# Second down projection in four groups of seven block products, with the weight sums made in HBM by GpSimd's transfers

## The reference

```python
x = x + jnp.concatenate([a, p], axis=-1) @ w_out[l]
h2 = rms_norm(x, norm2_g[l])
x = x + (jax.nn.silu(h2 @ w_gate[l]) * (h2 @ w_up[l])) @ w_down[l]
```

## Time and profile before

| what | us |
|---|---|
| median of three runs | 802.08 (802.04 to 802.59) |
| the profiled execution | 801.26 |
| its span | 799.8 |
| PE busy in the span | 793.5 |
| DVE, ACT, POOL busy | 625.5, 456.3, 88.8 |
| second down projection, from its first to its last matmuls | 57.3 |

### The profile page before, as it was taken

How to read it: one execution, slowest core, us unless ns; L and a number is a source line. 1 busy time by engine, 2 the same in 40 slices (tenths; PEclk the granted TensorE clock), 3 DMA queues, 4 the chain that set the end, 5 groups by cost and what they waited for, 6 DMA issues and landing times.

```text
span 799.8 us, 13164 instructions
## 1 busy us (share of the span) xinstructions
PE 793.5 (99%) x5158; PEld 696.3 (87%) x5158; DVE 625.5 (78%) x1037; ACT 456.3 (57%) x738; POOL 88.8 (11%) x77
## 2 busy tenths in 40 slices
PE   8999999999999999999999999999999999999998
PEld 6888888999888888899999998887778888888886
DVE  6889998785555766679999997486866898787977
ACT  6676677454535544456656563456665566555552
POOL 0001000010011202101101110011100333011100
PEclk9999999999999999999999999999999999999999
DMA  9655564557433556475687655464425666884321
GB/s 316 189 166 169 178 228 146 143 146 226 126 116 96 173 168 202 163 240 179 192 253 242 224 187 209 162 206 161 156 79 148 198 207 213 291 285 159 108 101 55
DMA packets 118126, 144.09 MB, mean 180 GB/s; under 512 B 11553, under 2 KB 86705, under 8 KB 117809
## 3 DMA queue, kind: packets, MB, share of 16 engines
q1 hardware_dynamic: 115616, 141.22, 54.9%
q10 hardware_dynamic: 2448, 2.03, 1.1%
HBM read 141.78 MB, written 1.46 MB: 179 GB/s over the span
## 4 chain that ended last, share of the span: by engine, by line
PE 97%; DVE 1%; DMA 1%; issue 0%; ACT 0%; SPq 0%; DVEq 0%; ACTq 0%
PE bank L654 94%; PE bank L770 1%; DMA panel_raw<-in_w_in 1%; DVE conv_acc L1788 1%; PE bank L1090 0%; PE bank L814 0%; PE bank L1039 0%; DVE panel_lo L1752 0%; PE bank L1063 0%; PE bank L867 0%; PE bank L792 0%; PE bank L969 0%; SPq L2607 0%; ACT panel_hi L1236 0%; DVE h L2213 0%
## 5 line engine op out<-in xcount | busy, mean ns | idle before, releaser
L1752 DVE TENSOR_TENSOR panel_lo<-panel_raw,panel_hi 128x1024 fp32r<-128x1024 f32 x237 | 299.9, 1268 | 109.2 <-ACT panel_hi L1236 107.2
L654 PE MATMUL bank<-x_halves,panel_hi 128*128 128x256 f32 (+1 forms) x1536 | 366.9, 321 | 0.7 <-DVE x_halves L2220 0.7
L1236 ACT ACTIVATE panel_hi<-panel_raw 128x1024 fp32r<-128x1024 f32 (+1 forms) x239 | 251.9, 1055 | 154.2 <-PE bank L654 152.1
L654 PE MATMUL bank<-x_halves,panel_lo 128*128 128x256 f32 x1024 | 288.3, 282 | 0.0
L654 PEld LDWEIGHTS bank<-x_halves,panel_hi 128*128 128x128 f32 x1536 | 255.8, 190 | 23.3 <-issue 0.9
L654 PEld LDWEIGHTS bank<-x_halves,panel_lo 128*128 128x128 f32 x1024 | 194.9, 190 | 0.2
L654 PE MATMUL bank<-panel_hi,x_halves 128*128 128x512 f32 x384 | 122.1, 399 | 0.0
L654 PEld LDWEIGHTS bank<-panel_hi,x_halves 128*128 128x128 f32 x384 | 70.0, 188 | 14.1 <-issue 0.3
L654 PE MATMUL bank<-panel_lo,x_halves 128*128 128x512 f32 x192 | 75.1, 391 | 0.0
L654 PE MATMUL bank<-panel_hi,act_hi 128*128 128x512 f32 x156 | 60.9, 390 | 0.0
L654 PE MATMUL bank<-panel_hi,act_lo 128*128 128x512 f32 x156 | 60.7, 389 | 0.0
(11 more groups left out here) (312 smaller groups left out, 1011.2 us busy)
## 6 DMA issues: line engine op xcount, KB each, us to landing
panel_raw<-in_w_in SPq DMA_DIRECT2D x35, 1024.0 KB, 5.3
panel_raw<-in_w_up SPq DMA_DIRECT2D x30, 1024.0 KB, 5.4
panel_raw<-in_w_down SPq DMA_DIRECT2D x16, 1024.0 KB, 5.0
panel_raw<-in_w_gate SPq DMA_DIRECT2D x10, 1024.0 KB, 5.5
panel_raw<-in_w_out SPq DMA_DIRECT2D x8, 1024.0 KB, 5.0
panel_raw<-in_w_in SPq DMA_DIRECT2D x11, 512.0 KB, 4.8
panel_raw<-in_w_branch_fox SPq DMA_DIRECT2D x4, 1024.0 KB, 5.0
panel_raw<-in_w_branch_gdn SPq DMA_DIRECT2D x4, 1024.0 KB, 5.0
```

What stands on the lines that cost most here:

```text
L654: return e.matmul(o, l, r, start=start, stop=stop, skip_group_check=True)
L1236: return e.activation(o, i_, ACT.Copy, scale=scale)
L1752: e.tensor_tensor(lo, raw_view(i, k0, kt), hi.bitcast(F32), ALU.subtract).then_inc(s_lo, 1)
```

## The change

There are four groups in place of two, so 16 of the 22 k-tiles are done by block products and 6 by plain halves. `HALVES` grows from 258 to 264, the list of panels shrinks from 130 to 126. `GROUP_ORDER` sets the seven products of a group without plain halves between them; a plain half stands ahead of each of the first two groups and four stand at the end.

DVE's adds of weight blocks are gone. The sums are made in HBM, in a scratch array `weight_sums`, by transfers that POOL issues: `copied` writes a block there, `added` accumulates another onto it. Each group has four stages with 2, 3, 2 and 1 transfers of 512 KB, 32 in all, 16 copies and 16 accumulations. `SUM_STEPS` gives the 16 half panels (12, 20, ... 92 and 142, 150, ... 174); at each, POOL waits until PE has multiplied that half and until the earlier stages of the same group have landed. Two groups take turns: (0,0), (1,0), (0,1), (1,1), ... then (2,0), (3,0), and so on.

SP loads 28 blocks, the raw ones and the sums, into ten buffers, the later ones as DVE is done with a buffer; a load of a sum waits for all sums of its half of the groups. `act2_sums` runs for eight tile pairs in place of four, with their splits on ACT and DVE.

```diff
--- before.py
+++ after.py
@@ -87,12 +87,20 @@
 
 
 
-GROUPS = 2
-DOWN2_ORDER = [(8, 0), (8, 1), (12, 0), (12, 1), (16, 0), (20, 0), (16, 1), (20, 1)]
+GROUPS = 4
+DOWN2_ORDER = [(16, 0), (16, 1), (20, 0), (20, 1)]
 BLOCKS = ("b11", "b12", "b21", "b22")
-GROUP_ORDER = [("b11", None, "b21", None, "b22", None, "t3", None, "t1", None, "t2", None, "t4", None),
-               ("b11", None, "b21", None, "b22", None, "t3", None, "t1", "t2", None, "t4", None, None)]
-ADDED_BEHIND = {"b11": "t1", "b21": "t3", "b22": "t2", "t3": "t4"}
+GROUP_ORDER = [(None, "b11", "b21", "b22", "t3", "t1", "t2", "t4"),
+               (None, "b11", "b21", "b22", "t3", "t1", "t2", "t4"),
+               ("b11", "b21", "b22", "t3", "t1", "t2", "t4"),
+               ("b11", "b21", "b22", "t3", "t1", "t2", "t4", None, None, None, None)]
+BLOCK_SEQ = [(g, b) for g, order in enumerate(GROUP_ORDER) for b in order if b]
+
+
+WEIGHT_SUMS = ("t1", "t3", "t2", "t4")
+SUM_ROUNDS = (2, 5, 7, 8)
+SUM_ORDER = [(g + i, r) for g in range(0, GROUPS, 2) for r in range(len(SUM_ROUNDS)) for i in range(2)]
+SUM_STEPS = [*range(12, 93, 8), *range(142, 175, 8)]
 BLOCK_BANK = {"b11": ("p1",), "b21": ("down2", 0, 0), "b22": ("down2", 1, 0), "t4": ("down2", 0, 1), "t1": ("p5",),
               "t2": ("p6",), "t3": ("p7",)}
 SUM_3, SUM_1, SUM_2, SUM_4 = range(4)
@@ -212,7 +220,8 @@
 TAPS_END = END["up", 1, KF // 2 - 1] + 1
 TAP_AT[TAPS_END] = TAP_AT.pop(TAPS_END + 1)
 TAIL_AT = {n: j for n, (s, j) in TAP_AT.items() if s == 1}
-BLOCKS_FROM = [END["up2", 1, 4], END["up2", 1, 6]]
+BLOCKS_FROM = END["up2", 1, 4]
+SUMS_AT = dict(zip(SUM_STEPS, SUM_ORDER))
 UP2_AT = {}
 for _j in range(KF // 2):
     for _s in range(2):
...
@@ -309,12 +318,12 @@
         poolT = at("poolT", [P, 4, T], 23.25)
         gain_final = at("gain_final", [P, D], 19.5)
         sq2 = at("sq2", [P, TT, 2, PW], 23.5)
-        block_at = [{"b11": 22, "b12": 22.5, "b21": 23, "b22": 23.5}, {"b11": 0, "b12": 0.5, "b21": 16.5, "b22": 21.5}]
-        block_raw = [{b: at(f"block_{b}_{i}", [P, HALF * PW], block_at[i][b]) for b in BLOCKS} for i in range(2)]
-        act_sums = [at(f"act_sums{i}", [P, 4, P], 21, skip=2048 * i) for i in range(2)]
+        block_at = (22, 22.5, 23, 23.5, 0, 0.5, 1, 1.5, 2, 2.5)
+        block_raw = [at(f"block{i}", [P, HALF * PW], unit) for i, unit in enumerate(block_at)]
+        act_sums = [at(f"act_sums{i}", [P, 4, P], 16.5, skip=2048 * i) for i in range(2)]
         act_sums_hi = at("act_sums_hi", [P, 2 * GROUPS, 4, P], 18, F32R)
-        act_sums_lo = at("act_sums_lo", [P, 2 * GROUPS, 4, P], 19.5, F32R)
-        sum_u, sum_v, minus_w, p5_less_v = [at(f"block_sum{i}", [P, WIDE], 1, skip=2048 * i) for i in range(4)]
+        act_sums_lo = at("act_sums_lo", [P, 2 * GROUPS, 4, P], 20, F32R)
+        sum_u, sum_v, minus_w, p5_less_v = [at(f"block_sum{i}", [P, WIDE], 10, skip=2048 * i) for i in range(4)]
         mixh, mixl = at("mix_hi", [P, KD, T], 11, F32R), at("mix_lo", [P, KD, T], 12, F32R)
         na_p = [at(f"na_p{i}", [P, TT, T], 13, skip=2048 * i) for i in range(4)]
         na_pT = [at(f"na_pT{i}", [P, TT, T], 14, skip=2048 * i) for i in range(HEADS)]
...
@@ -596,24 +605,27 @@
...
-            return w.rearrange("(k r p) c -> r p k c", r=2, p=P)[r]
+            return w.rearrange("(k r p) c -> r k p c", r=2, p=P)[r]
+
+        def sum_rows(g, t_):
+            return scratch_w[g, WEIGHT_SUMS.index(t_)].rearrange("(k p) c -> k p c", p=P)
+
+        def block_source(g, b):
+            return (block_rows(g, b) if b in BLOCKS else sum_rows(g, b)).rearrange("k p c -> p k c")
 
...
-        KEPT_IN = {b: b for b in BLOCKS} | {"t1": "b11", "t3": "b12", "t2": "b22", "t4": "b21"}
-        OTHER = {"t1": "b12", "t3": "b22", "t2": "b11", "t4": "b22"}
-        ADDS = list(ADDED_BEHIND.values())
+        def block_buffer(g, b):
+            return block_raw[BLOCK_SEQ.index((g, b)) % len(block_raw)]
+
+        def block_sem(q):
+            return s_block[q // 2 % len(s_block)]
 
         def block_landed(g, b):
-            return s_block[g][int(b[1]) - 1], 32
-
-        def block_added(g, b):
-            return s_block_add, len(ADDS) * g + ADDS.index(b) + 1
-
-        def block_ready(g, b):
-            return block_landed(g, b) if b in BLOCKS else block_added(g, b)
+            q = BLOCK_SEQ.index((g, b))
+            return block_sem(q), 16 * sum(block_sem(i) is block_sem(q) for i in range(min(q | 1, len(BLOCK_SEQ) - 1) + 1))
 
         def rows_of(sums, h0, n):
             src = scratch_c[sums]
@@ -1241,9 +1253,9 @@
                 i, k0, kt = HALVES[n - 1]
                 if i is None:
                     g, b = k0, kt
-                    e.wait_ge(*block_ready(g, b))
+                    e.wait_ge(*block_landed(g, b))
                     e.wait_ge(s_half, n - 4)
-                    copy(whi[(n - 1) % 4], block_raw[g][KEPT_IN[b]]).then_inc(s_hi, 1)
+                    copy(whi[(n - 1) % 4], block_buffer(g, b)).then_inc(s_hi, 1)
                     return
                 e.wait_ge(*raw_landed(i))
                 if n > 4:
@@ -1717,7 +1729,7 @@
...
-                if n == TOUCHES["p1",][-1]:
+                if n == TOUCHES["p1",][-1] + 3:
                     e.wait_ge(s_block_sums, 1)
                     copy(sum_u, bank_of(("p1",))).then_inc(s_u_copied, 1)
             out_rows = out[0].rearrange("(t p) d -> p t d", p=P)
@@ -1726,15 +1738,6 @@
 
 
         def vector_program(e):
-            def add_block(g, b, n):
-                t_ = ADDED_BEHIND[b]
-                to = block_raw[g][KEPT_IN[t_]]
-                e.wait_ge(*block_landed(g, OTHER[t_]))
-                e.wait_ge(s_lo, n)
-                if ADDS.index(t_):
-                    e.wait_ge(s_block_add, len(ADDS) * g + ADDS.index(t_))
-                e.tensor_tensor(to, to, block_raw[g][OTHER[t_]], ALU.add).then_inc(s_block_add, 1)
-
             def split(n):
                 if n > STEPS:
                     return
@@ -1743,10 +1746,7 @@
                 e.wait_ge(s_hi, n)
                 if i is None:
                     g, b = k0, kt
-                    e.tensor_tensor(wlo[w], block_raw[g][KEPT_IN[b]], whi[w].bitcast(F32), ALU.subtract) \
-                        .then_inc(s_lo, 1)
-                    if b in ADDED_BEHIND:
-                        add_block(g, b, n)
+                    e.tensor_tensor(wlo[w], block_buffer(g, b), whi[w].bitcast(F32), ALU.subtract).then_inc(s_lo, 1)
                     return
                 hi, lo = (panel_view(x[w], PLAN[i][2], 0, kt) for x in (whi, wlo))
                 e.tensor_tensor(lo, raw_view(i, k0, kt), hi.bitcast(F32),
...
@@ -2536,11 +2536,38 @@
                 e.wait_ge(s_sums, 3 * j + 2)
                 e.tensor_tensor(s_[:, SUM_4, :], x_[:, 2, :], s_[:, SUM_2, :], ALU.add).then_inc(s_sums, 1)
 
+            def copied(g, t_, b):
+                e.dma_start(sum_rows(g, t_), block_rows(g, b)).then_inc(s_weight_sums[g % 2], 16)
+
+            def added(g, t_, what):
+                e.dma_start(sum_rows(g, t_), what, accum_op=ALU.add, max_dma_last_dim=4 * WIDE) \
+                    .then_inc(s_weight_sums[g % 2], 16)
+
+            def weight_sums(n, g, stage):
+                e.wait_ge(s_half, n)
+                done = SUM_ROUNDS[-1] * (g // 2) + (SUM_ROUNDS[stage - 1] if stage else 0)
+                if done:
+                    e.wait_ge(s_weight_sums[g % 2], 16 * done)
+                if stage == 0:
+                    copied(g, "t1", "b11")
+                    copied(g, "t3", "b12")
+                if stage == 1:
+                    added(g, "t1", block_rows(g, "b12"))
+                    added(g, "t3", block_rows(g, "b22"))
+                    copied(g, "t2", "b22")
+                if stage == 2:
+                    added(g, "t2", sum_rows(g, "t1"))
+                    copied(g, "t4", "b21")
+                if stage == 3:
+                    added(g, "t4", sum_rows(g, "t2"))
+
             e.memset(minus_half, -0.5).then_inc(s_minus_half, 1)
             e.wait_ge(s_minus_half, 1)
             e.wait_ge(s_mean, 1)
             power(rsq[:, 0:2], 2).then_inc(s_rms, 1)
             for n in range(1, STEPS + 1):
+                if n in SUMS_AT:
+                    weight_sums(n, *SUMS_AT[n])
                 if n == 27:
                     e.wait_ge(s_consts, 16)
                     mask_key_bias(0)
@@ -2602,6 +2629,11 @@
                     e.dma_start(dst[:, :, s * n:(s + 1) * n], w_rows(weights[w], k0, kt, c0 + s * apart, n)) \
                         .then_inc(raw_landed(i)[0], 16)
 
+            def fetch_block(q, g, b):
+                if b not in BLOCKS:
+                    e.wait_ge(s_weight_sums[g % 2], 16 * SUM_ROUNDS[-1] * GROUPS // 2)
+                e.dma_start(block_view(block_raw[q % len(block_raw)]), block_source(g, b)).then_inc(block_sem(q), 16)
+
             x_rows = a["x"][0].rearrange("(t p) d -> p t d", p=P)
             for c in range(2):
```

(19 more changed lines are left out.)

9 lines of the change are left out of this document (5 added, 4 removed).

## The result

The changed kernel takes 853.8 us, before 802.2: a ratio of 1.0637 (95% interval 1.0618 to 1.0656), **51 us slower**. The forecast was 2.2 us faster. The profiled execution has a span of 851.0 us against 799.8.

What follows compares the result with a forecast made beforehand. PE's matmuls were taken to bound the kernel (busy 793.5 of 799.8 us). Terms -2.73 + 0.1 + 0.4 + 0 = -2.2 on the 802.08 median gave 799.8 us, range 799.0 to 807.0.

Steps and rivals of the forecast that it cites:

- The price of a matmul and the count: Second down projection: 240 matmuls in place of 252, at 0.2274 us each, a gain of 2.73 us.
- The back-to-back blocks: Second down projection: 21 block products without a half between, one every 1.36 us; stall of 0 to 0.2, taken as 0.1.
- the unknown i: Time POOL needs to issue one weight-sum transfer: 0.58, 1.30 or 2.84 us; 0.4 us of stall taken at half 84.
- the prediction's cheaper case: Half 84: later gate products keep clear of DVE and take 1.30 us each, so PE loses only 2i - 2.6.
- rival 1: GpSimd's issue of transfers is dear: stall of 0.9 to 4.0 us at half 84, total 800.4 to 803.5; chance 0.20.
- rival 2: Weight sums on two DMA engines hold up the panels: +12 us, about 811 (803 to 820); chance 0.22.
- its deciding point: Panels landing late by 11 us or more, from which PE loses time; at 14 us, 3 us per first accumulation.
- the 11 us that a panel has in hand: Cover of a panel between landing and PE's start on it: 5.6 us before ACT, 5.6 after, 11.2 us.
- a half share of the engine: A panel with half of a shared DMA engine takes 6.0 us, lags 0.6 a panel and never reaches 11.
- The third share: A panel with a third of a shared DMA engine takes 9.0 us against 5.44, losing 3.5 us a panel.
- The 36 us: Duration of an accumulation on two DMA engines when it has two thirds of each; about four panels lag meanwhile.
- The wait that the prediction looked for: Waits of ACT and PE for panel_raw between 100 and 600 us, with panels landing after 9 us or more.

Runs made afterwards that it cites:

- the kernel with the two moves: Changed kernel with all sum transfers' rows outermost, plus stage at half panel 92 moved to 104 and first group's plain half behind t3: 800.1 us, 0.9977 of before.

## Why the prediction was wrong

**Where it was right.** The price of a matmul and the count: the stage from the end of half panel 230 to the last matmul went from 57.3 to 54.8 us, and 54.7 was forecast. The back-to-back blocks held their 1.36 us, with one stall of 0.36 us at half panel 238, beside GpSimd's product (0.2 was expected there). The blocks' loads were never late, and the added sums of activations cost nothing. POOL's issue, the unknown i, is here:

```profile
317.00 2.26 POOL L2540 DMA_DIRECT2D weight_sums<-in_w_down  x2 [9.71 <-PE bank L666]
340.53 2.11 POOL L2540 DMA_DIRECT2D weight_sums<-in_w_down  x2 [21.27 <-PE bank L666]
342.65 2.54 POOL L2592 TENSOR_TENSOR gate_g<-gate_g,gate_f 128x512 f32<-128x512 f32 x2
...
342.21 5.20 DVE L1752 TENSOR_TENSOR panel_lo<-panel_raw,panel_hi 128x1024 fp32r<-128x1024 f32 x2
```

About 1.1 us for a copy, and at half 84 the products took 1.27 each. They did not run clear of DVE, as the prediction's cheaper case had it: of the two low parts in the DVE row one took 4.07 us in place of 1.22, beside these products. PE waited for neither, and rival 1 fell. The Trainium skill ("DMA: Bandwidth & Descriptors", "Specifications") gives about 1 us to the first byte for a transfer issued in software. These rows show 1.1 us, but of another thing, the time for which POOL is taken.

**The step that failed** is the weight of rival 2 and its price. In the sum the transfers stand at 0.4 us, by the sentence "By themselves they cost PE nothing unless POOL is late for something"; they cost 52.7. The prediction had the mechanism as a rival, two engines for a transfer whose outer dimension is two, and even its deciding point, but gave it a chance of 0.22 and 12 us. Three things in it were wrong.

First, the chance. The argument against it was the 11 us that a panel has in hand and a half share of the engine, 6.0 us a panel. The rows show what a panel really got during a first accumulation, here the one of the third group, in ACT's timeline:

```profile
378.04 1.06 ACT L1248 ACTIVATE panel_hi<-panel_raw 128x1024 fp32r<-128x1024 f32 x1 [4.02 <-DMA panel_raw<-in_w_up]
385.02 1.06 ACT L1248 ACTIVATE panel_hi<-panel_raw 128x1024 fp32r<-128x1024 f32 x1 [3.31 <-DMA panel_raw<-in_w_up]
395.37 2.00 ACT L1248 ACTIVATE panel_hi<-panel_raw 128x1024 fp32r<-128x1024 f32 x2 [7.83 <-DMA panel_raw<-in_w_up]
```

Panels come 7 and 10 us apart where PE uses one in 5.44. The third share (9.0 us) was the right one, not the half. On this the Trainium skill was plain ("DMA: Bandwidth & Descriptors", "Why a DMA increments its semaphore by 16 and not by 1"): the largest number up to 16 that divides the slowest dimension on both sides, hence 2 for these. The trace agrees, with 3.7 engines for two copies, and so does the run with an outer dimension of 128. The exception that the page allows for some copies didn't apply here. The prediction set a stated rule against a guess and gave the guess the better odds.

Second, it priced the accumulations of each group by themselves. The 36 us was near (POOL's slowest landing was 40.5 us), and the fourth group's, at half panel 142 with no other group's beside them, cost 3 us at half panels 153 to 155, as priced. But those of the first two groups met:

```profile
109.66 1.38 POOL L2498 TENSOR_TENSOR key_bias<-key_bias,constants 128x128 f32<-128x128 f32 x2 [33.30 <-DMA key_bias<-gate_sums]
110.98 3.89 POOL L2543 DMA_DIRECT2D weight_sums<-in_w_down  x2
...
124.24 1.87 POOL L2543 DMA_DIRECT2D weight_sums<-in_w_down  x1 [8.28 <-PE bank L666]
150.41 1.87 POOL L2543 DMA_DIRECT2D weight_sums<-in_w_down  x1 [24.30 <-issue]
```

The stages of half panels 28 and 36 are 24.8 us apart as they fall due (99.4 and 124.2), less than the 36 us. POOL's own program brought them closer: it is in order and stood 33 us for `key_bias`, so that the first began at 110.98. And the second accumulation of the stage of 36 then stood 24.3 us for nothing that the profile shows, and was issued at 150.41, in the middle of the delta rule's round trip. The prediction looked at what POOL's transfers delay on POOL, and not at what delays them.

Third, and the largest single part of the error: slack was measured on the panels alone. The panels are the transfers with the most in hand, 11 us. The 16 KB pieces of the delta rule's blocks have none, as DVE stands behind them in order. That one step lost 21 of the 51 us, and none of the prediction's rows had it. The way back of the same blocks, `XT` from `blocks_inverted`, held PE for another 4.1 us. The wait that the prediction looked for, ACT's and PE's for panels, is there too: the 11 us at half panels 98 to 101, of which 6.5 are two waits of PE behind late panels, and smaller ones behind 150.

On top of the waits come 12.6 us for the clock, which the prediction did not price at all, since PE never stood long enough before to show it. A slip without weight: 801.26 - 2.2 is 799.1, and not the 798.9 that the sum gives for a profiled execution.

**The sum as it turned out:** waits 40.1, clock 12.6, and -1.5 for the change without its sums (798.3 against 799.8: 2.5 less in the last stage, about 1 more ahead of it, nearly all of that the wait at half panel 56): 51.2, the difference of the two spans.

## What to carry to other kernels

Before a transfer is added, look at the outermost dimension of both its sides as the instruction carries it: with two there, half a megabyte sat on about two DMA engines and took 17.9 us to land (the median), and transfers that spread over all of them landed later; with the rows outermost the same bytes cost 2 us instead of 53. Measure slack on the transfers that have the least of it, small round trips that an in-order engine waits on, and not on the big streams that are loaded far ahead. And a place by number in an engine's program is the earliest time only: what stands ahead of it on that engine can push one such place towards the next.

## What the runs showed of the hardware

A transfer from a two-k-tile source was also cut up differently: POOL's queue carried 35328 packets with the k-tiles outermost, 6656 with the rows, and 20992 where either the copies or the accumulations alone were spread, for 17 MB in all of them; its share of the engines' time was 10.4% at the most and 9.4% at the least. A PE that stood for 19.2 us came back with the granted clock at the lower of its two levels (1.2 and 2.4 GHz): 0.50 from 178.3 to 182.3, and 0.41 in place of 0.28 us for a matmul. All such stretches together are put at 12.6 us of the 52.7. Whether a short wait does the same differed: after the 1.5 us at half panel 56, the granted clock from 197 to 205 was 0.79 in the kernel with the two moves and 1.00 in the second profile of the kernel before:

```profile
197.00:205.00 8.00, 7.90 (x109) 7.49 (x109) 3.80 (x10) 4.37 (x11) 0.00 (x0) 0.79 0.46 157
```

```profile
197.00:205.00 8.00, 8.00 (x113) 7.14 (x109) 2.80 (x5) 5.74 (x13) 0.00 (x0) 1.00 0.16 52
```
